# Reordering the first microseconds of a one-core encoder trunk: weights on ScalarE's queue, the norm's row on GpSimd's, high parts first

## The reference

```python
h = rms_norm(x, norm_mix)
proj = h @ w_in                    # q_a k_a v_a q_b k_b v_b u_c and the gate logits
o_a = chunked_rel_attention(q_a, k_a, v_a, q_norm_a, k_norm_a, rel_bias_a)
o_b = stick_breaking_attention(q_b, k_b, v_b)
o_c = multiscale_pool(u_c, w_pool, pool_scale)
merged = sig(g_a)*(o_a @ w_branch_a) + sig(g_b)*(o_b @ w_branch_b) + sig(g_c)*(o_c @ w_branch_c)
x = x + merged @ w_out
x = x + conv_gated_mlp(rms_norm(x, norm_ffn), w_up, conv_w, conv_b, w_down)
```

## Time and profile before

| what | value |
|---|---|
| median of 3 runs | 816.08 us (815.91 to 817.07) |
| the profiled execution | 815.84 us |
| its span, first to last instruction | 814.2 us |
| PE busy | 807.6 us, 99% of the span |
| DVE busy | 638.9 us, 78% |
| ACT busy | 418.2 us, 51% |
| POOL busy | 23.6 us, 3% |
| matmuls and transposes on PE | 3808 |

### The profile page before, as it was taken

One profiled execution on the slowest core, in us unless ns is written; L12 is line 12 of the kernel. 1 busy time (PEld: TensorE's weight loads), 2 busy tenths in 40 slices (PEclk: granted clock), 3 DMA queues, 4 the chain that ended last, 5 costly groups with the idle time before them and its releaser, 6 DMA issues.

```text
span 814.2 us, 11415 instructions
## 1 busy us (share of the span) xinstructions
PE 807.6 (99%) x3808; PEld 669.3 (82%) x3808; DVE 638.9 (78%) x944; ACT 418.2 (51%) x587; POOL 23.6 (3%) x38
## 2 busy tenths in 40 slices
PE   8999999999999999999999999999999999999998
PEld 6888888888888888888878888888888888888886
DVE  5958888867668675668688868777777788898797
ACT  6547676656645644334356564433443344566653
POOL 0010010000000060000000000000000000000000
PEclk9999999999999999999999999999999999999999
DMA  6342333312222224365637322666565555576455
GB/s 212 105 131 78 91 91 86 95 52 79 77 77 77 66 78 142 92 206 179 192 121 232 104 77 83 201 206 204 185 202 193 181 179 195 163 220 211 150 181 174
DMA packets 131071, 115.37 MB, mean 142 GB/s; under 512 B 6260, under 2 KB 109656, under 8 KB 129888
## 3 DMA queue, kind: packets, MB, share of 16 engines
q1 hardware_dynamic: 130048, 112.47, 44.0%
q0 software_dynamic: 672, 2.12, 1.0%
q10 hardware_dynamic: 320, 0.40, 0.2%
HBM read 101.31 MB, written 13.65 MB: 141 GB/s over the span
## 4 chain that ended last, share of the span: by engine, by line
PE 94%; DVE 3%; issue 1%; DMA 1%; ACT 0%; SPq 0%; DVEq 0%; ACTq 0%
PE ps L1829 29%; PE ps L1830 29%; PE ps L1831 29%; PE ps L1951 2%; PE ps L1942 2%; PE ps L1966 1%; PE ps L1965 1%; DMA x_in<-in_x_dram 1%; DVE suffix L1285 1%; DVE w_lo L1109 1%; PE ps L2147 0%; PE ps L1866 0%; DVE out_sb L1814 0%; PE ps L1925 0%; PE ps L1926 0%
## 5 line engine op out<-in xcount | busy, mean ns | idle before, releaser
L1829 PE MATMUL ps<-h_lo,w_hi 128*128 128x512 f32 x704 | 277.0, 393 | 0.1
L1830 PE MATMUL ps<-h_hi,w_hi 128*128 128x512 f32 x704 | 274.3, 390 | 0.0
L1831 PE MATMUL ps<-h_hi,w_lo 128*128 128x512 f32 x704 | 274.2, 390 | 0.0
L1109 DVE TENSOR_TENSOR w_lo<-w_raw,w_hi 128x1024 fp32r<-128x1024 f32 x104 | 128.2, 1232 | 68.0 <-ACT w_hi L620 33.8
L1829 PEld LDWEIGHTS ps<-h_lo,w_hi 128*128 128x128 f32 x704 | 132.2, 188 | 28.3 <-DVE w_lo L1109 0.7
L1831 PEld LDWEIGHTS ps<-h_hi,w_lo 128*128 128x128 f32 x704 | 132.2, 188 | 27.8
L1830 PEld LDWEIGHTS ps<-h_hi,w_hi 128*128 128x128 f32 x704 | 132.3, 188 | 26.1
L620 ACT ACTIVATE w_hi<-w_raw 128x1024 fp32r<-128x1024 f32 x72 | 76.3, 1059 | 139.6 <-PE ps L1831 139.5
L614 ACT ACTIVATE w_hi<-w_raw 128x1024 fp32r<-128x1024 f32 x32 | 33.9, 1060 | 62.7 <-PE ps L1831 59.6
L1677 DVE TENSOR_TENSOR conv_in<-ps,r_ffn 128x512 f32<-128x512 f32 x44 | 30.4, 690 | 22.5 <-PE ps L1831 22.2
L1028 ACT ACTIVATE conv_out<-conv_in,par 128x512 f32<-128x512 f32 x44 | 35.5, 807 | 9.7 <-DVE conv_in L1677 9.7
(11 more groups left out here) (283 smaller groups left out, 1356.5 us busy)
## 6 DMA issues: line engine op xcount, KB each, us to landing
w_raw<-in_w_in_dram SPq DMA_DIRECT2D x103, 256.0 KB, 3.1
w_raw<-in_w_up_dram SPq DMA_DIRECT2D x88, 256.0 KB, 3.2
raw_t<-in_w_down_dram SPq DMA_DIRECT2D x9, 1024.0 KB, 8.9
down_sums<-t_sum SPq DMA_DIRECT2D x9, 1024.0 KB, 5.7
w_raw<-in_w_down_dram SPq DMA_DIRECT2D x33, 256.0 KB, 3.0
w_raw<-down_sums SPq DMA_DIRECT2D x33, 256.0 KB, 3.8
raw_o<-in_w_out_dram SPq DMA_DIRECT2D x6, 512.0 KB, 4.8
w_raw<-down_sums SPq DMA_DIRECT2D x22, 128.0 KB, 2.9
```

The costliest lines, as they stand in the source:

```text
L1109: v.tensor_tensor(w_lo[:, slot, :], w_raw[:, slot, :], r32(w_hi[:, slot, :]), ALU.subtract)\
L1829: mm3(dst, l_hi, r_lo, start=start, stop=False, **kw)
L1830: mm3(dst, l_hi, r_hi, start=False, stop=False, **kw)
L1831: return mm3(dst, l_lo, r_hi, start=False, stop=stop, **kw)
```

## The change

Five things change, all in the first 14 us.

- **Queues.** The first half of the first unit's weights, which stood second on SP's queue between token tiles 0 and 1, becomes the first transfer of ACT's queue. The norm's row, which was the first of ACT's queue, becomes the first instruction of POOL.
- **POOL's order.** Behind that transfer, `ident` is cleared before `rows`.
- **ACT and DVE.** Both split half 0 of the weights ahead of token tile 0, where they did the tokens first.
- **PE's warm matmuls.** `WARM` goes from (3, 4) to (4, 2): six instead of seven.
- **PE's order.** The products of the first unit are issued by a new function: `hi x hi` first, which needs no low part, then `hi x lo` of the weights, then `lo x hi`, each with its own wait. The order of work is transposes 0, warm, products (kk 0, t 0), transposes 1, products (1, 0), transposes 2, products (0, 1), transposes 3, products (1, 1), then tiles 2 and 3. Before, transposes 1 came ahead of the first product, and products of tile 1 behind all transposes.

```diff
-WARM = (3, 4)
+WARM = (4, 2)
...
             x_load(0, 0)
-
-            sp.dma_start(w_raw[:, 0, 0:WB], win_v0[:, 0, :]).then_inc(first_landed, 16)
             for t in range(1, TT):
                 x_load(t, 0)
...
         def _(pool):
+            pool.dma_start(g_row[:, :], norm_mix[0].rearrange("(k c) -> k c", c=P)).then_inc(gmix_landed, 16)
+            pool.memset(ident[:, :], 0.0).then_inc(const_step, 1)
             pool.memset(rows[:, :, :], 0.0).then_inc(rows_zero, 1)
-            pool.memset(ident[:, :], 0.0).then_inc(const_step, 1)
...
-            a.dma_start(g_row[:, :], norm_mix[0].rearrange("(k c) -> k c", c=P)).then_inc(gmix_landed, 16)
+
+            a.dma_start(w_raw[:, 0, 0:WB], win_v0[:, 0, :]).then_inc(first_landed, 16)
             for r in (slice(0, HD), slice(HD, P)):
                 a.dma_start(w_raw[r, 0, WB:UNIT], win_v0[r, 1, :]).then_inc(w_landed[0], 16)
...
-            xt_split_hi(0, 0)
             a.wait_ge(gmix_ready, 1)
             first_hi(0).then_inc(first_hi_ready, 1)
+            xt_split_hi(0, 0)
             first_hi(1).then_inc(hi_ready, 1)
...
             d.wait_ge(gmix_ready, 1)
-            xt_split_lo(0, 0)
             d.wait_ge(first_hi_ready, 1)
             first_lo(0).then_inc(first_lo_ready, 1)
+            xt_split_lo(0, 0)
             d.wait_ge(hi_ready, N_VA + 1)
             first_lo(1).then_inc(lo_ready, 1)
...
+            def first_products(kk, t):
+
+
+                bank, tk, c = V_A_BANKS[t], slice(t * P, t * P + P), slice(kk * WB, kk * WB + WB)
+                pe.wait_ge(xt_hi_ready, t + 1)
+                if t == 0:
+                    pe.wait_ge(hi_ready if kk else first_hi_ready, 1)
+                mm3(ps[:, bank, :], xt_hi[:, kk, tk], w_hi[:, 0, c], start=kk == 0, stop=False)
+                if t == 0:
+                    pe.wait_ge(lo_ready if kk else first_lo_ready, 1)
+                mm3(ps[:, bank, :], xt_hi[:, kk, tk], w_lo[:, 0, c], start=False, stop=False)
+                pe.wait_ge(xt_lo_ready, t + 1)
+                return mm3(ps[:, bank, :], xt_lo[:, kk, tk], w_hi[:, 0, c], start=False, stop=False)
+
             x_transposes(0, 0)
             warm(1)
+            first_products(0, 0)
             x_transposes(1, 0)
-            for t in range(TT):
-                pe.wait_ge(xt_lo_ready, t + 1)
-                for kk in range(2):
-                    if t == 0:
-                        pe.wait_ge(lo_ready if kk else first_lo_ready, 1)
-                    last = value_product(V_A_BANKS[t], kk, t, slice(kk * WB, kk * WB + WB), 0)
-                    if t == 0:
-                        x_transposes(kk + 2, 0)
+            first_products(1, 0)
+            x_transposes(2, 0)
+            first_products(0, 1)
+            x_transposes(3, 0)
+            first_products(1, 1)
+            for t in (2, 3):
+                first_products(0, t)
+                last = first_products(1, t)
             last.then_inc(unit_done, 1)
```

## The result

The changed kernel takes 819.83 us (median of 7 runs), the kernel before 816.77 in the same comparison: a ratio of 1.0039, 95% interval 1.0030 to 1.0049, so 3.1 us slower. I had forecast 815.6, in a range of 814.8 to 817.0. One of the seven executions took 4669.82 us; nothing else in this study looks like it, and its cause is unknown.

The account below looks back on a forecast made before the run. PE was taken as the bound: three products moved forward (0.7 us) less 0.2 in gaps gain 0.5, so 815.84 - 0.5 = 815.3, plus 0.24 to the median gives 815.6 us, range 814.8 to 817.0.

Parts of the forecast that it names:

- What bounds the kernel: Whole kernel: PE, busy 99% of the span; the change is worth how far the next stage's start, 14.07, moves.
- The norm's row: 4 KB transfer on POOL: begun at 0.88, lands at 3.6, at worst 4.4, before PE asks at 4.18.
- Slowed by the 0.5 MB in flight: Rival at the row's transfer: lands at 4.6 to 4.9, PE stands 0.4 to 0.7 us, 816.1; chance 0.25.
- The row is very late: Rival at the row's transfer: POOL's first transfer costs over 2 us more, time 818; chance 0.03.
- The clock: Rival at PE's first products: 1.2 GHz stays, 0.43 instead of 0.23 each, 817.6, half near 816.8; chance 0.12.
- Transfers: First loads on two queues: tile 0 and first weights land at about 4.4, the weights' second half at 6.2.
- PE: First unit on PE: first product at 6.35, next stage at 13.6 instead of 14.07, 0.5 us gained.
- the gap of half 1: Before products (1, 0): the weights' half 1 is split by 7.85, where transposes 1 also end.
- Does it last?: After the first unit: no later stage hangs on a fixed moment, so all 0.5 us reach the end.
- The step from the profile to the median: Whole-kernel time: the runs' median stands 0.24 above the profiled execution, so 815.3 becomes 815.6.

Follow-up runs that it names:

- d: Changed kernel with SP and ACT holding back all their transfers until the norm's row has landed; 820.01 us, run once for its profile.
- h: Changed kernel with 11 warm matmuls instead of 4 ahead of the norm's transpose; 818.44 us, ratio to before 1.0019.
- f: Changed kernel with all three transfers as before, so only the order of splits and products and the warm matmuls change; 816.41 us, ratio to before 0.9999.
- j: Changed kernel with the norm's row at the head of SP's queue, first weights still heading ACT's; 816.91 us, ratio to before 1.0004.
- b: Kernel before with only the norm's row moved to the head of POOL's queue; 818.19 us, ratio to before 1.0018.
- i: Changed kernel with the first weights back in second place on SP's queue, norm's row still on POOL; 817.95 us, ratio to before 1.0017.
- g: Kernel before with only the first weights moved, to second place on ACT's queue behind the norm's row; 820.14 us, ratio to before 1.0043.
- c: Changed kernel with 15 warm matmuls instead of 4 ahead of the norm's transpose; 818.81 us, ratio to before 1.0024.
- a: Changed kernel with the norm's row back at the head of ACT's queue, ahead of the weights; 819.73 us, ratio to before 1.0035.

## Why the prediction was wrong

- **What bounds the kernel** held. 14.07 is the number to watch, and span less next stage is the same 800.1 us in all kernels.
- **The failed step is "The norm's row"**: "I take 2.7, with 2.6 and 3.5 as bounds. Begun at 0.88 it lands at 3.6, at worst 4.4." It began at 1.43 and took 6.1, landing at 7.52. The bounds came from two POOL transfers at 43 and 46 us. The first had 0.52 MB of SP's before it, of which 0.46 moved in 1.7 us; the second had next to nothing. The change puts 0.92 MB before the row, just when the queues start: by the table above it waits until 0.84 MB are moved, 4.0 us. I summed such bytes for the tiles, from the earlier trace rows, and never for the row. "Slowed by the 0.5 MB in flight" did stand among the rivals, but at 0.4 to 0.7 us of standing still, where 3.39 came.
- **"The row is very late"** was thus the case that came, with a chance of 0.03 and for another reason than the one I gave it: not a slow first transfer (d). Its 818 was still 1.8 us too low.
- **The clock**, the rival on the other side, came too, as a consequence. PE stood still for 3.4 us, the products ran at the low level, and that is 0.9 to 1.0 of the 3.1 us (h). I had tied it to two warm matmuls less; f, which has these, loses little by it.
- **"Transfers"**: with both large transfers at 0.9 us I had them share and land at 4.4. In j the earlier one landed at 3.8, the other at 5.0; in the changed kernel tile 0 landed 4.1 and the weights 4.3 after their issue, about 5.0 and 5.2. The landing was put 0.6 to 0.8 us too early. The weights' second half, which I had at 6.2, held ACT until 7.35 even in j.
- **"PE", the gain of 0.5 us**: the order alone gives 0.0 in the median (interval -0.7 to +0.7 us). The first product came where I put it (6.19 for 6.35), the gap of half 1 was mis-sized: with the transfers of before its split ended at about 9.0 in f, not at 7.85, and two products were at the low clock.
- **"Does it last?"** held: every microsecond at the start is one at the end.
- **The step from the profile to the median.** "The median of the runs stands 0.24 above that execution" came from three runs. The larger sets have it 0.6 to 0.9 above, so 815.6 was 0.3 to 0.7 too low before any mechanism was wrong.

The medians add up only in part. The row on POOL costs 1.5 us (b and i), the weights at the head of ACT's queue with the row in time 0.5 (j), an amount its interval does not tell from none, both together 2.9 to 3.1. The rest, 0.9 to 1.1, is their meeting: more bytes stand before the row and its landing takes another 1.0 to 1.7 us.

Open: whether POOL's packets wait for their turn at the transfer engines, or the fetching of their descriptors does. The traces show only that none moved while the bytes issued earlier did. Open too is why the granted clock is lower in five of g's executions.

## What to carry to other kernels

A small transfer that everything waits for belongs at the head of a hardware queue, first in time among all queues; a price taken from another moment is a price for the bytes that stood before it there, so sum what will have been issued on all queues and not yet moved. Fixing one late transfer shows nothing until the next late one is fixed too, so look at each landing on its own, in the order of issue over all queues. And when PE must stand and wait near the start, constant matmuls up to the expected landing are worth it (here 0.9 to 1.0 us). Four too many held the transpose back by 1.0 us in c's profile; the medians of c and h, 2.1 and 2.0 over before, don't tell them apart.

## What the hardware showed that I had not expected

- The same 4 KB on POOL's queue lands after 2.0, 2.8, 4.1, 4.8 or 6.1 us, and its first packet passes once 0, 0.17, 0.56, 1.48 or 0.84 MB of the other queues have moved; on ACT's queue at the head, the norm's row was there before PE asked at 3.75.
- A POOL whose first instruction is a transfer starts it at 1.43, where its first clearing started at 0.87: 0.56 us more at the start of the program.
- 256 KB on ACT's queue take 2.9 us when issued first (j), 4.3 beside SP's first tile (changed), 5.1 to 5.4 when issued 0.6 us later behind two of SP's tiles (a, g).
- The moment of the upper clock wanders between executions of one program: spacing 0.23 from 10.9 or from 13 us in the changed kernel, and from 5.2 or from 7.5 us in h and c, whose PE work is the same until then. Whether this makes the scatter of 815.8 to 818.6 of the kernel before is not shown: only one of its executions was profiled.
